# A fused two-block network: the second half of each weight unit becomes a plain difference, one unit in six moves to GpSimd, and a unit's first products come first

## The chip, the core and the metric

The kernel runs on one core of one Trainium2 chip. A core has five engines that run side by side, each through its own list of instructions in a fixed order: TensorE (PE, matrix products; its weight loads are shown apart as PEld), VectorE (DVE), ScalarE (ACT), GpSimd (POOL) and SyncE (SP, which here only issues transfers). They wait for each other on semaphores. SBUF is the on-chip memory of 128 partitions, PSUM the eight banks into which TensorE adds up products. The metric is the time of one execution on the device in microseconds.

## The reference

The program computes two transformer-like blocks on 256 tokens of width 2048, in float32. The large work is dense products with weights that are read once from HBM; between them stand small per-head products.

```python
# first block (one layer)
h = rms_norm(x, ln1); proj = h @ w_in                  # 2048 x 15376
y_a = gated_deltanet(...) @ w_branch_a                 # 8 heads of 128, chunks
y_b = moba_attention(...) @ w_branch_b                 # softmax attention, 8 heads
x = x + (sigmoid(gate_a) * y_a + sigmoid(gate_b) * y_b) @ w_out
u = causal_dwconv(rms_norm(x, ln2) @ w_up, ffn_conv, bias)
x = x + (silu(u_gate) * u_val) @ w_down; x = rms_norm(x, final_norm)
# second block (two layers)
shift, scale, gate = split(silu(c) @ w_mod[l] + b_mod[l])
h = rmsnorm(x) * (1 + scale) + shift; proj = h @ w_in_2[l]
y = concat(sparse_attention(...) * silu(g_a), groupnorm(retention(...)) * silu(g_b)) @ w_out_2[l]
x = x + gate * y
```

## The kernel before, in words

**Units.** Every dense product W·x is cut into blocks of 512 output columns and these into units of 128 x 1024 weights (`CH`), some 800 in all. A unit's path: SyncE starts a transfer of 512 KB into a slot of `ring` (or into a lent part of `AR` or `X`). ScalarE writes the rounded first half, `w1 = round(128 W)`, into a slot named `w` (`scalar_program.split`, recorded at L1431). VectorE writes the second half, `w2 = round(129 W - w1)`, over the raw weights (`vector_program.split`, recorded at L1881 as `ring_r<-ring,w`). TensorE then takes 16 products of 256 columns (orientation CM, weights stationary) or 8 of 512 (TM, activations stationary).

**Two products in place of one.** The fast float32 form of TensorE (`fp32r`, tiles named `_r`) rounds its inputs. So both operands are split in two: the activations into `x1 = round(x / 129)` and `x2 = x - 128 x1` (`first` and `second`; in `hhi`/`hlo` for the normed input), the weights into `w1` and `w2`. The block's sum is the sum of x1·w1 and x2·w2. In `gemm_part` the two products of one tile stand next to each other, first x1·w1, then x2·w2, and the unit begins with a wait for `w2_done`.

**Order of the work.** A planner in Python writes one list `steps` (sends, splits, units, phases of small jobs) and every engine runs its part in that order. Splits are put as far ahead as slots allow (`look_ahead`: 6 slots for `w1`, 9 for raw weights, plus lent ones). Between units come the phases of small jobs, a set number of units apart (`PAUSES`), and 192 units of `w_mod` for the second block's modulation, which VectorE alone multiplies and adds (`macc<-ring,sm,macc`, 128x1024).

**Small jobs that the change touches.** *Attention* (`moba` 4 jobs, `sparse` 8 jobs of two heads each): VectorE takes the row sums' reciprocals, ScalarE scales four identities by them (`inverse_sums`, `stg<-cst,sm`), and TensorE transposes and divides at once by six plain float32 products per job (`attend`, `ps<-stg,AR`). *Gated delta rule* (`gdn`, 4 jobs): TensorE spreads the cumulative decay and `bk` over rows (eight products), ScalarE copies the second to SBUF (`br`), GpSimd multiplies the matrix `AT` by it (`at`, recorded at L2478), and a doubling scheme inverts a triangular matrix. GpSimd also serves the masks of `gdn` (`AR<-AR,lev`), the relative-position bias (`AR<-AR` 128x1024 int32), rotary sums and the indexer.

## Time and profile before

| | us |
|---|---|
| median of 3 runs | 1954.91 (1953.28 to 1960.38) |
| the profiled execution's own time | 1957.05 |
| its span, first to last instruction | 1955.2 |
| PE busy | 1857.7 (95%) |
| PEld busy | 1738.3 (89%) |
| DVE busy | 1698.6 (87%) |
| ACT busy | 1233.6 (63%) |
| POOL busy | 228.9 (12%) |
| read from HBM | 531.50 MB, 273 GB/s over the span |

Busy time is the time in which an engine has at least one instruction under way. Products overlap in TensorE's pipeline (a product of 256 columns is drawn 0.28 us long while the next starts after 0.12 us), so TensorE's pace is read from starts and not from durations. A plain float32 product is recorded as two matmuls, an `fp32r` product or a transpose as one. A helper's line stands for all its uses: L151 is every product, L1431 every ScalarE copy, L1881 every three-operand VectorE instruction, L2478 every two-operand GpSimd instruction. All instructions of one name are then told apart by their tiles and shapes.

### The profile page before, as it was taken

What the parts mean: (1) busy time and instruction counts of PE and PEld (TensorE: products, weight loads), DVE (VectorE), ACT (ScalarE), POOL (GpSimd) and SP (SyncE); (2) the same over time, 40 slices, a digit from 0 to 9 for tenths busy, and PEclk for the clock granted to TensorE, in tenths of its full rate; (3) what the DMA queues carried; (4) which work ended last, traced back from release to release, by engine and by line L of the source; (5) the groups of instructions that cost most, each with busy time, mean ns of one, the idle gap of its engine ahead of it and who ended that gap; (6) DMA issues with size and microseconds to landing.
All of it is one profiled execution on the core that took longest, in us unless ns stands there. A gap on an engine that the chain in (4) does not pass through costs nothing.

```text
span 1955.2 us, 33776 instructions
## 1 busy us (share of the span) xinstructions
PE 1857.7 (95%) x13206; PEld 1738.3 (89%) x13206; DVE 1698.6 (87%) x2200; ACT 1233.6 (63%) x1911; POOL 228.9 (12%) x144
## 2 busy tenths in 40 slices
PE   6999999999999999899999999899999989998998
PEld 5888799999997899889998997898888879988887
DVE  7887997988798799999999997898888889897886
ACT  6667654744664674656765666755667775656773
POOL 0000041042010001222000000042210003232000
PEclk9999998999999999899999999999999999999999
DMA  8887776868898897688989997777788868786985
GB/s 287 261 271 248 258 241 218 286 211 276 302 356 318 283 309 241 223 289 294 318 308 344 331 328 244 273 255 255 246 267 307 272 222 301 227 278 209 331 290 183
DMA packets 258523, 535.82 MB, mean 274 GB/s; under 512 B 23608, under 2 KB 28733, under 8 KB 257341
## 3 DMA queue, kind: packets, MB, share of 16 engines
q1 hardware_dynamic: 257933, 531.44, 80.2%
q8 instruction: 105, 1.72, 0.3%
q10 hardware_dynamic: 432, 2.23, 0.3%
q14 instruction: 53, 0.43, 0.1%
HBM read 531.50 MB, written 2.10 MB: 273 GB/s over the span
## 4 chain that ended last, share of the span: by engine, by line
PE 41%; DVE 13%; ACT 5%; issue 4%; POOL 1%; DMA 1%; ACTq 0%; DVEq 0%; SPq 0%
PE ps L151 41%; DVE ring_r L1881 4%; ACT w L1431 2%; DVE macc L1881 2%; DVE AR_r L1881 1%; POOL AR L2478 1%; DMA ring<-in_w_in 1%; ACT stg L1437 1%; DVE stg L1873 1%; DVE AR L1873 1%; DVE stg L1881 1%; DVE AR L1881 1%; ACT L1437 1%; DVE stg L1878 0%; ACT stg L1431 0%
## 5 line engine op out<-in xcount | busy, mean ns | idle before, releaser
L151 PE MATMUL ps<-hh_r,w 128*128 128x256 f32 (+1 forms) x3500 | 865.5, 288 | 12.0 <-DVE ring_r L1881 6.8
L151 PE MATMUL ps<-hlo,ring_r 128*128 128x256 f32 x3116 | 758.9, 285 | 0.0
L1881 DVE SCALAR_TENSOR_TENSOR ring_r<-ring,w 128x1024 fp32r<-128x1024 f32 x495 | 621.5, 1275 | 115.6 <-ACT w L1431 114.4
L151 PEld LDWEIGHTS ps<-hh_r,w 128*128 128x128 f32 (+1 forms) x3500 | 671.2, 192 | 19.3 <-DVE ring_r L1881 8.1
L1431 ACT ACTIVATE w<-ring 128x1024 fp32r<-128x1024 f32 x495 | 511.3, 1055 | 179.0 <-PE ps L151 84.7
L151 PEld LDWEIGHTS ps<-hlo,ring_r 128*128 128x128 f32 x3116 | 596.7, 192 | 0.9 <-issue 0.5
L151 PE MATMUL ps<-w,AR_r 128*128 128x512 f32 x608 | 240.2, 395 | 2.7 <-DVE AR_r L1881 2.7
L151 PE MATMUL ps<-hlo,AR_r 128*128 128x256 f32 (+1 forms) x900 | 223.9, 287 | 0.0
L1881 DVE SCALAR_TENSOR_TENSOR AR_r<-AR,w 128x1024 fp32r<-128x1024 f32 (+1 forms) x150 | 187.7, 1262 | 34.0 <-ACT w L1431 33.6
L151 PE MATMUL ps<-ring_r,AR_r 128*128 128x512 f32 x520 | 203.8, 392 | 0.0
L151 PE MATMUL ps<-AR 128*128 128x64 f32 (+5 forms) x1340 | 182.7, 298 | 21.2 <-DVE AR L1877 10.9
L151 PEld LDWEIGHTS ps<-AR 128*128 128x128 f32 (+1 forms) x1340 | 166.8, 198 | 31.2 <-issue 15.9
L1431 ACT ACTIVATE w<-AR 128x1024 fp32r<-128x1024 f32 (+1 forms) x150 | 154.3, 1045 | 59.9 <-PE ps L151 34.2
L1881 DVE SCALAR_TENSOR_TENSOR macc<-ring,sm,macc 128x1024 f32<-128x1024 f32 x130 | 176.3, 1356 | 1.2 <-DMA ring<-in_w_mod 1.2
L151 PEld LDWEIGHTS ps<-hlo,AR_r 128*128 128x128 f32 (+1 forms) x900 | 174.1, 193 | 0.1
L2478 POOL TENSOR_TENSOR AR<-AR,stg 128x512 f32<-128x512 f32 (+1 forms) x41 | 66.2, 1632 | 734.2 <-DVE stg L1878 568.3
L151 PE MATMUL ps<-AR_r 128*128 128x512 f32 (+1 forms) x480 | 149.9, 363 | 0.0
L151 PE MATMUL ps<-hh_r,AR_r 128*128 128x256 f32 (+1 forms) x596 | 149.0, 288 | 0.9 <-DVE hlo L1881 0.9
L151 PEld LDWEIGHTS ps<-w,AR_r 128*128 128x128 f32 x608 | 115.0, 189 | 26.9 <-DVE ring_r L1881 2.5
L151 PEld LDWEIGHTS ps<-ring_r,AR_r 128*128 128x128 f32 x520 | 98.5, 190 | 20.1
L151 PEld LDWEIGHTS ps<-hh_r,AR_r 128*128 128x128 f32 (+1 forms) x596 | 114.1, 191 | 2.5 <-issue 2.3
L1881 DVE SCALAR_TENSOR_TENSOR ring_r<-ring,AR_r 128x1024 fp32r<-128x1024 f32 x81 | 104.6, 1293 | 13.2 <-ACT AR_r L1431 13.0
(223 smaller groups left out, 2475.4 us busy)
## 6 DMA issues: line engine op xcount, KB each, us to landing
ring<-in_w_in SPq DMA_DIRECT2D x314, 512.0 KB, 5.0
ring<-in_w_mod SPq DMA_DIRECT2D x141, 512.0 KB, 5.8
ring<-in_w_up SPq DMA_DIRECT2D x126, 512.0 KB, 5.5
ring<-in_w_down SPq DMA_DIRECT2D x66, 512.0 KB, 5.9
ring<-in_w_out SPq DMA_DIRECT2D x64, 512.0 KB, 5.5
AR<-in_w_in SPq DMA_DIRECT2D x63, 512.0 KB, 5.4
AR<-in_w_up SPq DMA_DIRECT2D x50, 512.0 KB, 5.4
AR<-in_w_mod SPq DMA_DIRECT2D x38, 512.0 KB, 5.9
```

The source lines that it names most:

```text
L151: return e.matmul(o, l, x, start=start, stop=stop, skip_group_check=True)
L1431: return e.activation(o, i, ACT.Copy, scale=scale)
L1437: return e.activation(o, i, f, scale=scale, **kw)
L1873: return e.tensor_tensor(o, a, b, op)
L1881: return e.scalar_tensor_tensor(o, a, s, b, op0, op1)
L2478: return e.tensor_tensor(o, a, b, op)
```

## The change

- The factor 129 (`SPK`) leaves the weights. ScalarE writes `w1 = round(128/129 W)`; the second half is the plain difference `w2 = W - w1`, a two-operand instruction. The activations carry the factor instead: the constants in the normalisations, in `gdn`, `moba`, `up`, `glu` and the residual are multiplied by it.
- Of the units of weights one in six (`i % SHARE == 3`) gets its second half from GpSimd, under a semaphore of its own (`w2_pool`), except around a block whose input is fresh (`fresh`: from two units ahead of it to nine behind its start). The changed program has 110 such instructions, all of 128x1024.
- `gemm_part` runs all first products of a unit, then waits for the second half and runs all second products.
- Attention: ScalarE divides the exponentials in place (`divided`), and TensorE transposes them against the identity, six single-pass transposes per job.
- `gdn`: the `bk` rows, ScalarE's copy `br` and GpSimd's product `at` go; `AT` is scaled by `bk` where VectorE forms it, and VectorE's preparations on two to four columns are rearranged.

```diff
 # tensor_program, gemm_part
-            e.wait_ge(*w2_done.after(j))
+            e.wait_ge(*w1_done.after(j))
...
                     for i in range(2):
-                        o, a = ps[i][:, 0:n], slice(128 * i, 128 * i + 128)
-                        fp(o, x1[:, a], b1[:, kk, :], k == 0, False)
-                        q = fp(o, x2[:, a], b2[:, kk, :], False, end)
+                        fp(ps[i][:, 0:n], x1[:, 128 * i:128 * i + 128], b1[:, kk, :], k == 0, False)
...
+            e.wait_ge(*(w2_pool if j in on_pool else w2_done).after(j))
+            for kk in range(m):
...
+                        q = fp(ps[i][:, 0:n], x2[:, 128 * i:128 * i + 128], b2[:, kk, :], False, end)
...
 # scalar_program, split
-            copy(wslot[j].at[:, 0:n], slot[j].at[0][:, 0:n], scale=SPL).then_inc(*w1_done.step(j))
+            copy(wslot[j].at[:, 0:n], slot[j].at[0][:, 0:n], scale=SPL / SPK).then_inc(*w1_done.step(j))
 # vector_program, split
+            if j in on_pool:
+                return
             e.wait_ge(*w1_done.after(j))
-            stt(rounded[:, 0:n], raw[:, 0:n], SPL + 1.0, wslot[j].at[:, 0:n], MUL, SUB).then_inc(*w2_done.step(j))
+            tt(rounded[:, 0:n], raw[:, 0:n], wslot[j].at[:, 0:n], SUB).then_inc(*w2_done.step(j))
 # GpSimd's program
+        def split(j):
...
+            if j in on_pool:
+                e.wait_ge(*w1_done.after(j))
+                tt(rounded[:, 0:n], raw[:, 0:n], wslot[j].at[:, 0:n], SUB).then_inc(*w2_pool.step(j))
 # planner
+    units = [j for j, c in enumerate(chunks) if c[0] == "w"]
+    fresh = [i for i, j in enumerate(units) if chunks[j][1]["fresh"] and chunks[j][2] == 0]
+    on_pool = {j for i, j in enumerate(units) if i % SHARE == 3 and all(not f - 2 <= i < f + 10 for f in fresh)}
 # attend (TensorE), inverse_sums -> divided (ScalarE)
-                fp(b0[:, 256 * h:256 * h + 128], L0[:, h, :], r0)
+                e.transpose(b0[:, 256 * h:256 * h + 128], L0[:, h, :], ident)
...
-            for u in range(4):
-                q = copy(quarter(st(J, "s"), u), ident, scale=rcol[:, u:u + 1])
+            for h in range(2):
+                copy(L0[:, h, :], L0[:, h, :], scale=rcol[:, h:h + 1])
+                q = copy(L1[:, h, :], L1[:, h, :], scale=rcol[:, 2 + h:3 + h])
 # gdn: TensorE, ScalarE, GpSimd
-                for u, h, n, c in G.U:
-                    q = fp(quarter(b, u), G.bk[:, u:u + 1].to_broadcast([128, 128]), ident)
...
-                copy(flat2(G.PP), b[:, :]).then_inc(*gdn_act.step("br", bt))
...
-                tt(flat2(G.AT), flat2(G.AT), flat2(G.PP), MUL).then_inc(*gdn_pool.step("at", bt))
```

TensorE at the program's first unit, bank by bank (`ps0`, `ps1` are the two banks of the block; `hh_r` is x1, `hlo` is x2, `w1` the first half, `ring_r` the second). Before:

```order
L151 MATMUL ps0<-hh_r,w1 128x256
L151 MATMUL ps0<-hlo,ring_r 128x256
L151 MATMUL ps0<-hh_r,w1 128x256
L151 MATMUL ps0<-hlo,ring_r 128x256
L151 MATMUL ps1<-hh_r,w1 128x256
L151 MATMUL ps1<-hlo,ring_r 128x256
L151 MATMUL ps1<-hh_r,w1 128x256
L151 MATMUL ps1<-hlo,ring_r 128x256
```

The same unit now:

```order
L152 MATMUL ps0<-hh_r,w1 128x256 x2
L152 MATMUL ps1<-hh_r,w1 128x256 x2
L152 MATMUL ps0<-hh_r,w1 128x256 x2
L152 MATMUL ps1<-hh_r,w1 128x256 x2
L152 MATMUL ps0<-hlo,ring_r 128x256 x2
L152 MATMUL ps1<-hlo,ring_r 128x256 x2
L152 MATMUL ps0<-hlo,ring_r 128x256 x2
L152 MATMUL ps1<-hlo,ring_r 128x256 x2
```

The count is the same; eight products now stand ahead of the first that needs the second half, and two products in a row no longer add to the same sum.

VectorE in the feed-forward stage, about 829 to 857 us of the trace before (`macc` is the modulation, `X<-ps,X` the half sums, `AR<-AR,cst` a step of the bias). Before:

```order
L1881 SCALAR_TENSOR_TENSOR AR_r<-AR,w 128x1024 x2
L1881 SCALAR_TENSOR_TENSOR ring_r<-ring,w 128x1024 x3
L1881 SCALAR_TENSOR_TENSOR macc<-ring,sm,macc 128x1024
L1881 SCALAR_TENSOR_TENSOR ring_r<-ring,AR_r 128x1024
L1881 SCALAR_TENSOR_TENSOR X<-ps,X 128x512 x2
L1877 TENSOR_SCALAR AR<-AR,cst 128x1024
L1881 SCALAR_TENSOR_TENSOR ring_r<-ring,w 128x1024 x3
```

Now:

```order
L1888 TENSOR_TENSOR AR_r<-AR,w 128x1024 x2
L1888 TENSOR_TENSOR ring_r<-ring,w 128x1024 x2
L1896 SCALAR_TENSOR_TENSOR macc<-ring,sm,macc 128x1024
L1888 TENSOR_TENSOR ring_r<-ring,AR_r 128x1024
L1896 SCALAR_TENSOR_TENSOR X<-ps,X 128x512 x2
L1892 TENSOR_SCALAR AR<-AR,cst 128x1024
L1888 TENSOR_TENSOR ring_r<-ring,w 128x1024 x2
```

Two of nine second halves have left VectorE's list here; the rest keeps its place.

GpSimd from the end of the merge (`stg<-stg,X`) into the feed-forward stage, the 12 bias steps being `AR<-AR` 128x1024. Before:

```order
L2478 TENSOR_TENSOR stg<-stg,X 128x512 x8
L2513 MEMSET AR 128x8
L2514 MEMSET AR 128x32
L2478 TENSOR_TENSOR AR<-AR 128x1024 x12
L2478 TENSOR_TENSOR AR<-AR,stg 128x256
```

Now:

```order
L2496 TENSOR_TENSOR ring_r<-ring,w 128x1024 x2
L2528 MEMSET AR 128x8
L2529 MEMSET AR 128x32
L2496 TENSOR_TENSOR ring_r<-ring,w 128x1024 x2
L2496 TENSOR_TENSOR AR_r<-AR,w 128x1024
L2496 TENSOR_TENSOR AR<-AR 128x1024
L2496 TENSOR_TENSOR ring_r<-ring,w 128x1024
L2496 TENSOR_TENSOR AR<-AR 128x1024
L2496 TENSOR_TENSOR AR_r<-AR,w 128x1024
L2496 TENSOR_TENSOR AR<-AR 128x1024
L2496 TENSOR_TENSOR ring_r<-ring,w 128x1024
```

The second halves stand between the bias steps, and each waits in GpSimd's list behind the step ahead of it.

## Rows read from the trace of the kernel before

**Rows 1.** The page: busy time of each engine; the chain that ended last, by engine.
```profile
PE 1857.7 (95%) x13206; PEld 1738.3 (89%) x13206; DVE 1698.6 (87%) x2200; ACT 1233.6 (63%) x1911; POOL 228.9 (12%) x144
PE 41%; DVE 13%; ACT 5%; issue 4%; POOL 1%; DMA 1%; ACTq 0%; DVEq 0%; SPq 0%
```

**Rows 2.** Busy time by stage: feed-forward; second block, layer one; layer two.
```profile
core 0: us, PE busy (x) PEld busy (x) DVE busy (x) ACT busy (x) POOL busy (x), PEclk, DMA share, GB/s
...
690.00:1160.00 470.00, 459.01 (x3333) 438.10 (x3332) 442.78 (x526) 294.97 (x397) 42.16 (x12) 0.98 0.86 298
1200.00:1550.00 350.00, 330.79 (x2344) 306.58 (x2343) 302.80 (x407) 237.34 (x403) 53.28 (x31) 0.97 0.79 263
1600.00:1900.00 300.00, 281.88 (x2085) 264.66 (x2084) 263.92 (x354) 201.68 (x341) 53.58 (x31) 0.98 0.81 269
```

**Rows 3.** Waits of TensorE: who for whom, us in total, times, longest.
```profile
PE ps L1088 <- DMA AR<-in_gdn_conv: 12.1, 1, 12.1
PE ps L151 <- ACT stg L1431: 8.3, 4, 2.5
PE ps L151 <- DVE ring_r L1881: 8.1, 4, 5.0
PE ps L151 <- DVE AR_r L1881: 7.3, 5, 3.1
```

**Rows 4.** Waits of VectorE, same columns.
```profile
DVE ring_r L1881 <- ACT w L1431: 114.4, 105, 3.8
```

**Rows 5.** Second halves on VectorE: count, min/median/max ns, first and last start.
```profile
L1881 DVE SCALAR_TENSOR_TENSOR ring_r<-ring,w x495: 1204/1222/2921, 16.4 to 1930.7; 128x1024 fp32r<-128x1024 f32 x165
```

**Rows 6.** In order of time, VectorE, then GpSimd: start, us, instruction.
```profile
450.35 1.22 DVE L1881 SCALAR_TENSOR_TENSOR ring_r<-ring,w 128x1024 fp32r<-128x1024 f32 x1
451.48 2.19 DVE L1881 SCALAR_TENSOR_TENSOR AR_r<-AR,w 128x1024 fp32r<-128x1024 f32 x1
453.59 2.18 DVE L1881 SCALAR_TENSOR_TENSOR macc<-ring,sm,macc 128x1024 f32<-128x1024 f32 x1
...
450.94 3.75 POOL L2478 TENSOR_TENSOR AR<-AR,lev 128x512 f32<-128x512 f32 x2 [4.23 <-PE ps L151]
```

**Rows 7.** The same, where VectorE reads PSUM meanwhile.
```profile
315.01 4.38 DVE L1881 SCALAR_TENSOR_TENSOR AR<-ps,VT,AR 128x253 f32<-128x253 f32 x11 [0.40 <-ACT AR L1431]
...
315.02 2.29 POOL L2478 TENSOR_TENSOR AR<-AR,lev 128x512 f32<-128x512 f32 x2 [5.72 <-PE ps L151]
```

**Rows 8.** The same in the feed-forward stage, GpSimd 1024 wide.
```profile
807.84 4.05 DVE L1881 SCALAR_TENSOR_TENSOR ring_r<-ring,w 128x1024 fp32r<-128x1024 f32 x2
...
792.79 6.21 POOL L2478 TENSOR_TENSOR AR<-AR 128x1024 int32<-128x1024 int32 x1 [21.68 <-DVE AR L1877]
808.00 2.81 POOL L2478 TENSOR_TENSOR AR<-AR 128x1024 int32<-128x1024 int32 x1 [9.00 <-DVE AR L1877]
```

**Rows 9.** TensorE in order of time: plain float32 products, then transposes.
```profile
237.73 3.62 PE L151 MATMUL ps<-AR 128*128 128x128 f32 x31
...
243.05 0.60 PE L1229 MATMUL ps<-cst,AR 128*128 128x128 f32 x4
243.49 0.60 PE L1232 MATMUL ps<-cst,AR 128*128 128x128 f32 x4
```

**Rows 10.** ScalarE: the four scaled identities; one pass over 256 columns.
```profile
1336.07 0.49 ACT L1437 ACTIVATE AR<-AR,sm 128x256 f32<-128x256 f32 x1
...
1340.05 1.27 ACT L1431 ACTIVATE stg<-cst,sm 128x128 f32<-128x128 f32 x4 [1.57 <-DVE sm L2071]
```

**Rows 11.** TensorE inside a unit, in order of time.
```profile
700.84 0.28 PE L151 MATMUL ps<-hh_r,w 128*128 128x256 f32 x1
700.96 0.28 PE L151 MATMUL ps<-hlo,AR_r 128*128 128x256 f32 x1
701.08 0.28 PE L151 MATMUL ps<-hh_r,w 128*128 128x256 f32 x1
```

**Rows 12.** GpSimd: groups by form; count, busy us, mean ns, idle before.
```profile
L2478 POOL TENSOR_TENSOR AR<-AR 128x512 f32<-128x512 f32 x5 | 7.4, 1476 | 311.2 <-DVE AR L1881 311.1
```

More of the change, by code:

```diff
@@ L167, with pauses @@
 }
+PLACES = {}
+SHARE = 6
+MODS = {}
+def pauses(job):
+    return PLACES.get((job.kind, *job.at), PAUSES.get(job.kind, ()))
 USES = {
@@ L443, in inline @@
         job = Job(kind, *at)
-        for seg in range(len(PAUSES.get(kind, ())) + 1):
+        for seg in range(len(pauses(job)) + 1):
             phase(job, seg)
     def enqueue(q, jobs, seg=0):
-        q.append([[(j, s, (PAUSES[j.kind] + (0,))[s]) for j in jobs
-                   for s in range(seg, len(PAUSES[j.kind]) + (j is jobs[-1]))],
-                  PAUSES[jobs[0].kind][seg - 1] if seg and PAUSES[jobs[0].kind] else 0])
+        q.append([[(j, s, (pauses(j) + (0,))[s]) for j in jobs
+                   for s in range(seg, len(pauses(j)) + (j is jobs[-1]))],
+                  pauses(jobs[0])[seg - 1] if seg and pauses(jobs[0]) else 0])
     def step_jobs():
@@ L598, in evacuate @@
                 enqueue(short, [job], 2)
-            elif kind != "ga" and len(PAUSES.get(job.kind, ())) > 0:
+            elif kind != "ga" and len(pauses(job)) > 0:
                 enqueue(short, [job], 1)
@@ L1066, in gemm_part @@
                 k = k0 + kk
-                end = k == kt - 1
                 if b["fresh"] and (k % 2 == 0):
@@ L1081, in gemm_part @@
                         fp(o, b1[:, kk, a], x1, k == 0 and ct % 2 == 0, False)
+            e.wait_ge(*(w2_pool if j in on_pool else w2_done).after(j))
+            for kk in range(m):
+                k = k0 + kk
+                end = k == kt - 1
+                x1, x2 = operand(b, k + b["k0"])
+                if b["orient"] == "TM":
+                    for i in range(2):
+                        q = fp(ps[i][:, 0:n], x2[:, 128 * i:128 * i + 128], b2[:, kk, :], False, end)
+                else:
+                    for ct in range(-(-n // 128)):
+                        a = slice(128 * ct, min(128 * ct + 128, n))
+                        o = ps[ct // 2][0:a.stop - a.start, 256 * (ct % 2):256 * (ct % 2) + 256]
                         q = fp(o, b2[:, kk, a], x2, False, end)
@@ L1567, in moba @@
             if seg == 3:
-                inverse_sums(J, rcol, moba_dve.after("recip", hp), moba_act.step("diag", hp))
+                divided(L0, L1, rcol, moba_dve.after("recip", hp), moba_act.step("diag", hp))
             if seg == 4:
@@ L1575, in moba @@
                 e.wait_ge(*moba_pe.after("pv", hp))
-                copy(st(J, "s"), pb(J, "f")[:, :]).then_inc(*moba_act.step("out", hp))
+                copy(st(J, "s"), pb(J, "f")[:, :], scale=SPK).then_inc(*moba_act.step("out", hp))
                 e.wait_ge(*moba_act.after("out", hp))
@@ L1658, in gdn @@
                 e.wait_ge(*gdn_dve.after("qk3", bt))
-                for u in range(4):
-                    q = copy(G.KX[:, u, :], quarter(b, u), scale=G.ksc[:, u:u + 1])
+                for u, h, n, c in G.U:
+                    q = copy(G.KX[:, u, :], quarter(b, u), scale=eg[:, 1, h:h + 1] if n else G.ksc[:, u // 2:u // 2 + 1])
                 q.then_inc(*gdn_act.step("kx3", bt))
@@ L1806, in sparse @@
             if seg == 3:
-                inverse_sums(J, rcol, sp_dve.after("recip", L, hp), sp_act.step("diag", L, hp))
+                divided(L0, L1, rcol, sp_dve.after("recip", L, hp), sp_act.step("diag", L, hp))
             if seg == 4:
@@ L1988, in rstd @@
                 e.wait_ge(*rstd_dve.after("gain0", n))
-                ts(gsp, gsc, 1.0 / (SPL + 1.0), MUL)
-                ts(shp, modcm[:, L, 0:16], 1.0 / (SPL + 1.0), MUL).then_inc(*rstd_dve.step("gain", n))
+                ts(gsp, gsc, 1.0 / SPK, MUL)
+                ts(shp, modcm[:, L, 0:16], SPK, MUL).then_inc(*rstd_dve.step("gain", n))
             e.wait_ge(*sumsq.after("sq", 4 if n == 2 else n, 1, 3))
@@ L2111, in bd_job @@
                 ts(gcn, two(pb(J, "b")[:, 0:16]), -1.0, MUL).then_inc(*bd_dve.step("gcn"))
-                e.wait_ge(*bd_act.after("eg"))
-                tt(beg, bet[:, 1, :], eg[:, 1, :], MUL).then_inc(*bd_dve.step("beg"))
         def conv(J, seg):
@@ L2139, in conv @@
                 e.wait_ge(*conv_act.after("root", *J.at))
[L2140 removed]
+                root = st(J, "z")[:, 0:4] if kind == "q" else krt[:, 4 * hp:4 * hp + 4]
+                e.reciprocal((rq if kind == "q" else rk)[:, 4 * hp:4 * hp + 4], root).then_inc(*conv_dve.step("inv", *J.at))
         def z_silu(J, seg):
@@ L2563, in pool_program @@
         for what, *a in steps:
-            if what == "phase" and a[0].kind in parts:
+            if what == "split":
+                split(*a)
+            elif what == "phase" and a[0].kind in parts:
                 parts[a[0].kind](*a)
```

81 lines of the change are left out of this document (38 added, 43 removed).

## Prediction

> **What bounds the kernel now.** I read the page first: TensorE is busy for 1857.7 of 1955.2 us, VectorE for 1698.6, and the chain that ended last runs for 41% through products and for 13% through VectorE [rows 1]. So there is a first engine with little idle time (97.5 us) and a second that is not far behind it. The reader is to see both numbers: a gain has to come out of TensorE's work or its waits, and a loss can come from VectorE. Then the stages: in the feed-forward stage VectorE is busy for 442.8 of 470 us, in the two layers of the second block for 302.8 of 350 and 263.9 of 300 [rows 2]. VectorE has 27.2, 47.2 and 36.1 us left there, about 6% in the first and 12% in the others.
>
> Then TensorE's waits. Waits for `ring_r`, which are those for a second half, are 8.1 us in 4 times; those for `AR_r` are 7.3 us in 5 times, and that name is also carried by activations [rows 3]. The largest single one, 12.1 us, is the start of the program, which the change does not touch [rows 3]. Seen from the other side, VectorE itself waited 105 times, 114.4 us in all, for ScalarE's first half before it could form a second one [rows 4]: most second halves are formed as early as the slots allow and lie ready before TensorE comes to them. The pace inside a unit: starts at 700.84, 700.96, 701.08, 0.12 us per product of 256 columns, no matter whether the next one adds to the same sum or to another [rows 11].
>
> **The plain difference.** The three-operand form takes 1222 ns at the median [rows 5], and the next 1024-wide one starts 1.13 us after it (450.35, 451.48) [rows 6]. The two-operand form of 128x1024 is not in the trace. It reads the same two tensors and writes the same one. Bounds: half the price at the one end (0.57 us, as if a pass were saved, which would take another 0.57 us from each of the 690 that stay on VectorE), 1.28 us at the other, the price of the other three-operand form beside it. The nearest row is the three-operand form itself, so I take its price: a difference of 0 us. ScalarE's instruction has another constant, 0 us. The factors in the activations sit in constants of instructions that stand there anyway, 0 us.
>
> **First products first.** No instruction comes or goes; TensorE may start a unit when the first half is there, and reaches the wait eight products later, 8 x 0.12 = 0.95 us [rows 11]. Only a unit that waited for its second half gains, at most 0.95 us: 4 such waits for `ring_r` give 3.8 us, and if all 5 of `AR_r` were second halves it would be 8.6 us [rows 3]. I take 4. It adds a wait in the middle of a unit; behind it on TensorE stands only the unit itself, and after it the small jobs that stood behind the unit before. Should alternating between sums have cost something, the pace would change; the rows show 0.12 us for both kinds of step, so 0.
>
> **Attention.** Twelve jobs with six plain float32 products each. The trace draws such a product as two matmuls, and 31 of them in a row take 3.62 us, so (3.62 - 0.28)/30 = 0.111 us apart [rows 9]. Transposes: four from 243.05, the next kind from 243.49, 0.11 us each, drawn once [rows 9]. So a job goes from 12 x 0.111 = 1.33 us to 6 x 0.11 = 0.66 us, and twelve save 8.0 us. ScalarE had four scaled identities in 1.27 us, 0.3 us apart [rows 10]; now it has two passes over 128 columns and two over 256 (0.49 us, 0.4 apart): 1.5 us, and TensorE, which waited 8.3 us in 4 times for them [rows 3], may wait 0.2 us longer each time. 12 x 0.2 = 2.4 us on ScalarE, which is busy for 63% of the span [rows 1]; less than 1 us of it counts.
>
> **Gated delta rule.** 16 broadcasts of `bk` go, 32 matmuls x 0.111 = 3.6 us of TensorE. Four `at` products on GpSimd go, of the kind that takes 1476 ns on average [rows 12], with four copies on ScalarE. They stand in a chain of dependent steps; if VectorE and TensorE come to the next step 1 us sooner in each job, that is 4 us. It lies between 0 (the step comes at its place in the list anyway) and 4 x 1.5 = 6; I take 4 with the broadcasts counted apart.
>
> TensorE's work thus falls by 8.0 + 3.6 = 11.6 us.
>
> **One unit in six on GpSimd.** 110 second halves leave VectorE: 110 x 1.13 = 124 us of its work. What GpSimd takes is the unknown. It takes 2.29 us for two products of 512 columns while VectorE reads PSUM, 1.15 each [rows 7]. Where VectorE reads two SBUF tensors it is another picture: GpSimd needs 3.75 us for two, and the VectorE instructions at 451.48 and 453.59 take 2.19 and 2.18 us in place of 1.22 and about 1.28 [rows 6]: VectorE stands still for 0.9 to 0.97 us while GpSimd has the inputs. At 1024 columns (int32) GpSimd takes 2.81 us, and two second halves that run beside it take 4.05 us, where 1.13 + 1.22 = 2.35 is the price alone: 1.7 us of standstill [rows 8]. So a 1024-wide difference on GpSimd would hold VectorE for 1.7 (the int32 row) to 1.94 us (twice the 512-wide 0.97), if VectorE comes with a two-tensor instruction just then, and for nothing if VectorE is idle or reads PSUM. Per unit VectorE's time changes by -1.13 at one end and by 1.94 - 1.13 = +0.81 us at the other; times 110 this is -124 to +89 us. VectorE is busy for 87% of the span and most of its work has two SBUF inputs, so I take three quarters of 1.94, 1.46 us, +0.33 per unit, +36 us. Of this only what falls on stretches in which VectorE is on the path counts, 13% of the span by the chain [rows 1]: about 5 us, and 6 with the worse timing of the small jobs. The other 30 us go into VectorE's idle time, of which the 114.4 us of [rows 4] are a part; without that cover they would all count.
>
> The Trainium skill has this as a rule and it speaks against the change: "SBUF — State Buffer", section "Who interferes with whom", says that a VectorE instruction with two SBUF inputs and a GpSimd instruction that reads SBUF exclude each other, and that the later one stands still for the whole of the other. The rows above agree in kind (0.97 and 1.7 us of standstill) [rows 6, 8]. The skill's "GPSIMD Engine Reference", section "Elementwise — side-by-side cycle accounting", gives 4497 ns for 2048 columns; an estimate from it for 1024 is 2.25 us, by which the worst case per unit would be +1.12 us and the whole +123 us of VectorE's time. The sum does not use it.
>
> A second cost: GpSimd can also come late. At 792.79 one step took 6.21 us instead of 2.81, since VectorE's instructions followed one another without a gap [rows 8]. The unit's second half is then ready some 5 to 6 us after the first. TensorE needs it later than that where the slots are full, so I count nothing; it is in rival A.
>
> **Sum.** -11.6 (products) - 4 (waits for second halves) - 4 (gated delta rule) + 6 (VectorE) = -13.6 us. Against the profiled execution's own 1957.05 us that is 1943.4; its time lies 2.1 us above the median of the three runs, 1954.91, so on their scale 1941.3, 0.7% less. What a measurement of this kernel can tell from no change I take as 0.5%, 9.8 us: 1945.1 and 1964.7 are the bounds.
>
> **Rivals.**
>
> A, slower: the standstill of VectorE decides. In the feed-forward stage some 37 units go to GpSimd; at the full +0.81 they add 30 us to a VectorE that has 27.2 us left [rows 2], and since the load comes in bunches I count 10 us. In the two layers of the second block 57 units add 46 us, of which half lands where TensorE waits for small jobs: 23 us. With the 19.6 us of gains it comes to 1955 + 33 - 19.6 = 1968, and to 1975 if late second halves add some. For it: [rows 6, 8]. Against: TensorE waits for a second half only a few times now [rows 3], so there is room. It decides once VectorE's work per stage passes the stage's length.
>
> B, a larger gain: TensorE's small-job waits come from a VectorE that is behind, and 110 instructions fewer in its list bring it forward. Of 97.5 us of idle time 85 are not the start; and the granted clock is 0.97 to 0.98 in the stages [rows 2], a 2% loss on 1955 us, some 40 us, that follows on idle time. A third of both is 28 + 13 = 41 us; with the 11.6 of products 1955 - 53 = 1902, say 1905. For it: the standstill is zero where VectorE is idle or reads PSUM [rows 7]. Against: most of VectorE's list reads two SBUF tensors.
>
> C, no difference: the products removed lie where TensorE waits for others anyway (41% of the chain is TensorE [rows 1]), so 5 of the 11.6 us count, the waits' 4 and the delta rule's 4 are eaten by VectorE's +8: 1955 - 5 = 1950.
>
> Chances: my forecast (1925 to 1945) 0.35; B 0.17; C (1945 to 1965) 0.25; A 0.23. So faster by over 0.5% 0.52, within 0.5% 0.25, slower 0.23. The range takes in B's number and A's 1975: 1903 to 1976; the likeliest case's own range is 1925 to 1945.
>
> **What would show it.** The products: `ps<-stg,AR` gone, 72 transposes in its place, each 0.11 us after the last. The price: TENSOR_TENSOR `ring_r<-ring,w` with a median of 1222 ns; a median well below overturns my zero. The standstill: its mean above its median, single ones at 3 us, and GpSimd instructions of 2.3 us alone and over 3 beside VectorE; VectorE's busy time near 1698.6 + 36 = 1735 us. If it falls below 1650, the 0.33 is wrong and B is near. TensorE's waits for `ring_r`: a few us at most. If they are over 20 us, or if a GpSimd-made second half heads the list of TensorE's waits, A holds. A pace other than 0.12 us inside a unit would make all of this wrong, as it would count some 12,000 times (800 units of 16 or 8 products).

## The result, and the profile after

| | before | after |
|---|---|---|
| median, us | 1956.35 (1953.28 to 1960.38, 4 runs) | 2010.96 (2010.05 to 2012.02, 4 runs) |
| ratio after to before | | 1.0278, 95% interval 1.0257 to 1.0299 |
| span of the profiled execution | 1955.2 | 2009.2 |
| mean granted clock of TensorE | 0.977 | 0.959 |

The change makes the kernel 54.6 us slower, where 13.6 us less was forecast. The page of the changed kernel, busy times and then the chain that ended last (they answer to [rows 1]):

```profile
PE 1868.5 (93%) x13102; PEld 1743.9 (87%) x13102; DVE 1723.1 (86%) x2089; ACT 1232.3 (61%) x1907; POOL 527.3 (26%) x250
PE 38%; DVE 15%; ACT 5%; issue 4%; POOL 3%; DMA 1%; ACTq 0%; DVEq 0%
```

Each page is of one execution. TensorE has 104 instructions fewer and is busy 10.8 us longer, at a lower granted clock; its idle time grew from 97.5 to 140.7 us. VectorE has 111 instructions fewer and is busy 24.5 us longer, yet its share of the span fell from 87 to 86%. The stages (same columns as [rows 2]; since the kernel is slower, the same stretch holds somewhat less work):

```profile
690.00:1160.00 470.00, 450.60 (x3224) 429.67 (x3224) 438.37 (x480) 287.43 (x388) 129.45 (x45) 0.97 0.83 285
1200.00:1550.00 350.00, 317.03 (x2172) 289.46 (x2173) 296.89 (x383) 223.94 (x388) 102.81 (x50) 0.95 0.76 253
1600.00:1900.00 300.00, 278.19 (x1975) 256.44 (x1974) 256.84 (x331) 191.12 (x327) 100.65 (x48) 0.98 0.78 254
```

VectorE is busy for 438, 297 and 257 of 470, 350 and 300 us: it has idle time in all three stages. TensorE's waits in the changed kernel (us in total, times, longest; they answer to [rows 3]):

```profile
PE ps L152 <- DVE macc L1896: 17.6, 6, 4.5
PE ps L1174 <- ACT AR L1452: 17.4, 5, 6.4
PE ps L152 <- DVE AR L1892: 16.9, 3, 9.1
PE ps L1113 <- DMA AR<-in_gdn_conv: 12.1, 1, 12.1
PE ps L152 <- ACT w L1452: 10.4, 4, 4.6
PE ps L1423 <- DVE stg L1888: 10.2, 5, 5.7
PE ps L152 <- DVE sm L2189: 7.2, 1, 7.2
```

The waits for `ring_r` are nearly gone (1.3 us, once). What grew are waits for small jobs: the end of the modulation (`macc`, 6.7 us before), the divided exponentials (`L1174`; 14.4 us in 6 times in the kernel without the share, which is introduced below), the bias and mask steps (`AR L1892`, 10.9 us in 2 times before). TensorE hardly waits for the second half of a unit; it waits for small jobs that stand behind second halves in VectorE's list.

The second halves themselves (count, min/median/max ns, first and last start), on VectorE and on GpSimd, beside [rows 5]:

```profile
L1888 DVE TENSOR_TENSOR ring_r<-ring,w x425: 1187/1217/3444, 16.4 to 1983.0; 128x1024 fp32r<-128x1024 f32 x142
L2496 POOL TENSOR_TENSOR ring_r<-ring,w x70: 2356/2691/7601, 50.5 to 1984.9; 128x1024 fp32r<-128x1024 f32 x70
```

The median is that of before (1217 against 1222 ns), the longest is 3444 ns. In order of time, VectorE and then GpSimd (start, us), to be read beside [rows 6]:

```profile
1005.63 4.58 DVE L1888 TENSOR_TENSOR ring_r<-ring,w 128x1024 fp32r<-128x1024 f32 x2
...
1006.17 2.95 POOL L2496 TENSOR_TENSOR ring_r<-ring,w 128x1024 fp32r<-128x1024 f32 x1 [11.02 <-ACT w L1452]
```

GpSimd comes in the middle of VectorE's first instruction, waits until it ends (2.95 in place of 2.36 us), and VectorE's second one stands still until GpSimd is done: the two take 4.58 us where 1.22 + 1.13 = 2.35 is their price, 2.2 us of standstill.

And what such a delay meets. The longest of TensorE's waits that grew is one for a bias step in the feed-forward stage. GpSimd, VectorE and TensorE in the changed kernel:

```profile
771.62 3.32 POOL L2496 TENSOR_TENSOR ring_r<-ring,w 128x1024 fp32r<-128x1024 f32 x1
...
772.66 2.82 DVE L1892 TENSOR_SCALAR AR<-AR,cst 128x1024 f32<-128x1024 int32 x1
...
775.63 3.59 PE L152 MATMUL ps<-AR 128*128 128x32 f32 x16 [9.11 <-DVE AR L1892]
```

The same step in the kernel without the share:

```profile
751.16 0.74 DVE L1892 TENSOR_SCALAR AR<-AR,cst 128x1024 f32<-128x1024 int32 x1
...
752.05 3.10 PE L152 MATMUL ps<-AR 128*128 128x32 f32 x16 [3.99 <-DVE AR L1892]
```

GpSimd's second half makes the step 2.1 us longer (2.82 against 0.74), and TensorE waits for just this step. It waits 5.1 us more in all; for the other 3 us VectorE came later to this place against TensorE, behind two more holds (a `ring_r` and a `macc` that started at 745.89 and 751.17 us).

A second place shows another way of being late. It is the longest wait for the divided exponentials, one attention job of the second block's first layer: VectorE, GpSimd, ScalarE and TensorE, each in order of time:

```profile
1392.28 3.42 DVE L1896 SCALAR_TENSOR_TENSOR macc<-AR,sm,macc 128x1024 f32<-128x1024 f32 x1
1395.62 1.75 DVE L1888 TENSOR_TENSOR AR_r<-AR,AR_r 128x1024 fp32r<-128x1024 f32 x1
1398.66 1.39 DVE L1896 SCALAR_TENSOR_TENSOR AR<-ps,sm,AR 128x128 f32<-128x128 f32 x4 [1.29 <-POOL AR L2496]
...
1402.30 1.00 DVE L1899 TENSOR_REDUCE sm<-AR 128x2 f32<-128x256 f32 x2
1403.33 0.17 DVE L1892 TENSOR_SCALAR sm<-sm 128x4 f32<-128x4 f32 x1
...
1391.24 3.38 POOL L2496 TENSOR_TENSOR ring_r<-ring,w 128x1024 fp32r<-128x1024 f32 x1
1394.58 3.95 POOL L2496 TENSOR_TENSOR AR<-AR,sel 128x256 f32<-128x256 f32 x2
...
1403.54 0.40 ACT L1458 ACTIVATE AR<-AR,sm 128x128 f32<-128x128 f32 x1 [9.67 <-DVE sm L1892]
...
1409.37 0.44 PE L1174 MATMUL ps<-cst,AR 128*128 128x128 f32 x1 [6.39 <-ACT AR L1452]
1409.60 0.42 PE L1175 MATMUL ps<-cst,AR 128*128 128x128 f32 x1
```

In the kernel without the share the same job reads:

```profile
1353.29 1.76 DVE L1896 SCALAR_TENSOR_TENSOR macc<-AR,sm,macc 128x1024 f32<-128x1024 f32 x1
1354.97 2.31 DVE L1888 TENSOR_TENSOR AR_r<-AR,AR_r 128x1024 fp32r<-128x1024 f32 x1
1357.21 1.21 DVE L1888 TENSOR_TENSOR ring_r<-ring,w 128x1024 fp32r<-128x1024 f32 x1
1358.34 1.38 DVE L1896 SCALAR_TENSOR_TENSOR AR<-ps,sm,AR 128x128 f32<-128x128 f32 x4
...
1352.24 3.96 POOL L2496 TENSOR_TENSOR AR<-AR,sel 128x256 f32<-128x256 f32 x2
...
1363.21 0.40 ACT L1458 ACTIVATE AR<-AR,sm 128x128 f32<-128x128 f32 x1 [6.51 <-DVE sm L1892]
...
1369.04 0.45 PE L1174 MATMUL ps<-cst,AR 128*128 128x128 f32 x1 [4.01 <-ACT AR L1452]
```

GpSimd's second half at 1391.24 makes the `macc` take 3.42 us, 2.1 more than its price. But here the hold is made good: VectorE has one second half less to form, and in the kernel without the share GpSimd's own product `AR<-AR,sel` holds the same two VectorE instructions (1.76 and 2.31 us). What is left is that this product now stands behind the second half in GpSimd's list and starts 3.4 us later against VectorE's `macc`, and VectorE waits for it for 1.29 us. From the `macc` to `AR<-ps,sm,AR` VectorE takes 6.38 us, and 5.05 without the share: this wait is the whole delay. Behind it stand the maxima (`TENSOR_REDUCE`), for whose result ScalarE sits idle, then the exponentials, the reciprocals and ScalarE's division, and TensorE waits for 6.39 us in place of 4.01. The rest of that difference is that TensorE came to the wait about 1 us sooner. So a share on GpSimd also delays GpSimd's own small jobs; what that is worth over the whole kernel is bounded below.

The reader is to see that VectorE can be late although it is busy for 86% only: its free time lies elsewhere. TensorE's last two rows also show its pace behind a wait of several us: the transposes start 0.23 us apart, where they are 0.11 apart in undisturbed jobs.

### The profile page after: what moved, and what is told of

The parts are those of the page before. It is cut to its first block, busy times and chain, and to the rows that moved or that the text cites. A ratio compares the mean times of both kernels' runs of the same rounds, so it can differ in the third digit from the quotient of the medians.

```text
span 2009.2 us, 33543 instructions
## 1 busy us (share of the span) xinstructions
PE 1868.5 (93%) x13102; PEld 1743.9 (87%) x13102; DVE 1723.1 (86%) x2089; ACT 1232.3 (61%) x1907; POOL 527.3 (26%) x250
## 4 chain that ended last, share of the span: by engine, by line
PE 38%; DVE 15%; ACT 5%; issue 4%; POOL 3%; DMA 1%; ACTq 0%; DVEq 0%
PE ps L152 38%; DVE ring_r L1888 4%; POOL AR L2496 2%; DVE macc L1896 2%; ACT w L1452 2%; DVE stg L1896 2%; DVE AR_r L1888 1%; DVE stg L1888 1%; ACT stg L1458 1%; DVE AR L1888 1%; DVE AR_r L1896 1%; DVE AR L1896 1%; DMA ring<-in_w_in 1%; ACT L1458 1%; DVE AR L1892 0%
## 5 line engine op out<-in xcount | busy, mean ns | idle before, releaser
L1888 DVE TENSOR_TENSOR ring_r<-ring,w 128x1024 fp32r<-128x1024 f32 x425 | 579.5, 1380 | 108.0 <-ACT w L1452 107.2
L152 PE MATMUL ps<-hh_r,w 128*128 128x256 f32 (+1 forms) x3500 | 511.5, 290 | 7.1 <-ACT w L1452 5.6
L152 PEld LDWEIGHTS ps<-hh_r,w 128*128 128x128 f32 (+1 forms) x3500 | 460.6, 194 | 15.1 <-ACT w L1452 7.2
L152 PE MATMUL ps<-hlo,ring_r 128*128 128x256 f32 x3116 | 442.0, 285 | 1.3 <-DVE ring_r L1888 1.3
L2496 POOL TENSOR_TENSOR ring_r<-ring,w 128x1024 fp32r<-128x1024 f32 x70 | 205.1, 2929 | 834.9 <-ACT w L1452 834.9
L152 PEld LDWEIGHTS ps<-hlo,ring_r 128*128 128x128 f32 x3116 | 405.8, 192 | 2.0 <-DVE ring_r L1888 1.9
L1888 DVE TENSOR_TENSOR AR_r<-AR,w 128x1024 fp32r<-128x1024 f32 (+1 forms) x128 | 181.2, 1426 | 36.2 <-ACT w L1452 36.1
L152 PE MATMUL ps<-hlo,AR_r 128*128 128x256 f32 (+1 forms) x900 | 128.5, 286 | 0.2 <-DVE AR_r L1888 0.2
L1888 DVE TENSOR_TENSOR ring_r<-ring,AR_r 128x1024 fp32r<-128x1024 f32 x74 | 104.2, 1411 | 17.3 <-ACT AR_r L1452 17.2
L1452 ACT ACTIVATE AR_r<-ring 128x1024 fp32r<-128x1024 f32 x81 | 85.2, 1055 | 31.8 <-PE ps L152 20.1
```

The source lines that it names most:

```text
L152: return e.matmul(o, l, x, start=start, stop=stop, skip_group_check=True)
L1452: return e.activation(o, i, ACT.Copy, scale=scale)
L1888: return e.tensor_tensor(o, a, b, op)
L2496: return e.tensor_tensor(o, a, b, op)
```

## The experiments

Theory 1: GpSimd's share costs the time, because it holds VectorE. Rivals: the order of products (2), the smaller jobs (3), and, within the share, that GpSimd's halves come late (1b). A narrower form of theory 1 is that a hold costs only where small jobs on VectorE stand in TensorE's way (1c). "Against before" is the median less that of the kernel before in the same batch. VectorE's busy time and TensorE's idle time (span less busy time) are from each one's profiled execution.

| run | against before, us | ratio, 95% interval | VectorE busy | TensorE idle |
|---|---|---|---|---|
| changed kernel | +54.6 | 1.0278 (1.0257 to 1.0299) | 1723.1 | 140.7 |
| no share | +1.0 | 1.0007 (0.9993 to 1.0021) | 1694.1 | 107.2 |
| share, old order | +58.0 | 1.0295 (1.0273 to 1.0316) | 1720.5 | 147.1 |
| no share, old order | +4.9 | 1.0021 (1.0010 to 1.0032) | 1694.0 | 111.7 |
| write only | -37.1 | 0.9806 (0.9792 to 0.9821) | 1568.7 | 84.3 |
| hold only | +94.7 | 1.0480 (1.0467 to 1.0494) | 1833.2 | 173.8 |
| added on VectorE | +69.4 | 1.0351 (1.0334 to 1.0369) | 1810.0 | 152.9 |
| one input | -19.5 | 0.9903 (0.9888 to 0.9917) | 1611.0 | 93.2 |
| quarters | +22.5 | 1.0122 (1.0107 to 1.0137) | 1689.9 | 123.8 |
| one in twelve | +18.0 | 1.0093 (1.0080 to 1.0106) | 1706.8 | 119.3 |
| calm stretches | +27.8 | 1.0148 (1.0132 to 1.0164) | 1719.9 | 123.7 |
| attention only | +1.9 | 1.0004 (0.9992 to 1.0016) | 1697.9 | 104.7 |
| transposes undivided | -0.9 | 0.9999 (0.9988 to 1.0010) | 1698.0 | 103.3 |
| delta rule only | +0.8 | 1.0006 (0.9998 to 1.0015) | 1695.0 | 104.2 |
| order only | -2.5 | 0.9982 (0.9973 to 0.9991) | 1698.4 | 98.5 |

**Share and order, two by two.**

```diff
-    on_pool = {j for i, j in enumerate(units) if i % SHARE == 3 and all(not f - 2 <= i < f + 10 for f in fresh)}
+    on_pool = set()
```

> The changed kernel, but VectorE forms every second half; all other edits stay. Theory 1 (GpSimd's share costs the time: its instructions hold VectorE, and the small jobs behind them come late to TensorE): the other terms of the prediction are left, so 1956.4 - 19.6 = 1937 us, between 1930 and 1950; VectorE's second halves have mean and median together near 1.25 us. Theory 2 (the order of the products inside a unit costs it, by late second halves or a worse stream on TensorE): still above 1990. Theory 3 (the smaller attention and delta-rule jobs start something later): still above 1990.

Without the share the kernel is at 1957.66 us: 53.6 of the 54.6 us belong to the share. The 19.6 us of other gains are missing too, which none of the theories had, so the time lies above the range of 1930 to 1950.

```diff
             e.wait_ge(*w1_done.after(j))
+            e.wait_ge(*(w2_pool if j in on_pool else w2_done).after(j))
...
-                        fp(ps[i][:, 0:n], x1[:, 128 * i:128 * i + 128], b1[:, kk, :], k == 0, False)
+                        o, a = ps[i][:, 0:n], slice(128 * i, 128 * i + 128)
+                        fp(o, x1[:, a], b1[:, kk, :], k == 0, False)
+                        q = fp(o, x2[:, a], b2[:, kk, :], False, end)
...
-            e.wait_ge(*(w2_pool if j in on_pool else w2_done).after(j))
...
```

> The changed kernel with the product order of before (first and second product of a tile next to each other, the unit waits for its second half at its start); GpSimd keeps its 110 units. Theory 1: 2011 or some us more, up to 2025, since GpSimd's late second halves now hold the whole unit. Theory 2: near 1955.

> The changed kernel without GpSimd's share and with the product order of before: only the plain difference, the constants and the smaller jobs are left. Theory 1: as without the share alone, plus the 4 us that the order was to bring, 1941 (1933 to 1953). Theory 2: 1940 too, but then the run without the share and with the new order is at 1990. Theory 3: above 1990.

The old order costs 3.4 us more with the share and 3.9 without: theory 2 falls. So does theory 3, since neither kernel without the share is near 1990. What is left without share and order (plain difference, constants, smaller jobs) was to bring 15.6 us and brings none: the kernel is 4.9 us slower than before.

**Hold or lateness.** In the first run GpSimd keeps its place, its waits and its signal, and reads nothing:

```diff
-                tt(rounded[:, 0:n], raw[:, 0:n], wslot[j].at[:, 0:n], SUB).then_inc(*w2_pool.step(j))
+                e.memset(rounded[:, 0:n].bitcast(F32), 0.0).then_inc(*w2_pool.step(j))
```

> The changed kernel, but GpSimd writes zeros to its 110 units' second half in place of the difference: it reads no SBUF; same place in its list, same wait, same signal. (What it leaves out: those units' second half of the weights.) Theory 1, in the form that VectorE's standstill costs the time: VectorE is not held and has 110 instructions less than without the share (1957.7), so 1957 or less, 1935 to 1960; VectorE's second halves beside GpSimd take 1.22 us. Theory 1b, GpSimd's halves come late (its place in the list, its waits): still above 1990.

1920.47 us, below even the range of 1935 to 1960: taking 110 second halves off VectorE is worth 38 us when nothing holds it. The changed kernel, which differs from this run in what GpSimd reads and in how long its instruction is, is 90.5 us slower (91.7, each against its own before). VectorE and GpSimd of the write-only run, at a place like the one above:

```profile
684.50 2.36 DVE L1888 TENSOR_TENSOR ring_r<-ring,w 128x1024 fp32r<-128x1024 f32 x2
...
685.45 0.96 POOL L2581 MEMSET ring_r<- 128x1024 f32 x1 [9.20 <-ACT w L1452]
```

Two second halves in 2.36 us with GpSimd's instruction across both: no standstill. In the second run VectorE forms all halves, and GpSimd reads at the same places for nobody:

```diff
+    on_pool = set()
+    extra = {j for i, j in enumerate(units) if i % SHARE == 3 and all(not f - 2 <= i < f + 10 for f in fresh)}
...
 # GpSimd's program
+            if j in extra:
                 e.wait_ge(*w1_done.after(j))
...
+                tt(spare[:, :].rearrange("p (a b) -> p a b", b=256), mid(cst[:, 0:256], 4), mid(cst[:, 0:256], 4), ADD).then_inc(*w2_pool.step(j))
```

> The changed kernel with every second half on VectorE, and at the 110 places GpSimd adds two tensors of 128x1024 (a constant, into a spare 16-bit buffer that nobody reads): the hold without relief and without lateness. If the hold of VectorE costs the time, it must be at or above the changed kernel's 2011, since 110 x 1.22 = 134 us of VectorE's work have come back as well: 2030 to 2100, VectorE's busy time above 1800. If lateness of GpSimd's halves is the cause: 1958, as without the share.

2052.27 us. No other engine waits for the result of these additions, so none of this is a late second half (1b): 110 two-input instructions on GpSimd that relieve nobody cost 93.7 us against the kernel without the share. GpSimd's own later jobs can still come late in this run. The third run puts the same instruction on VectorE:

```diff
 # vector_program, behind its own second half, in place of GpSimd's program
+            if j in extra:
...
+                tt(spare[:, :].rearrange("p (a b) -> p a b", b=256), mid(cst[:, 0:256], 4), mid(cst[:, 0:256], 4), ADD).then_inc(*w2_pool.step(j))
```

> The changed kernel without the share, and at the same 110 places VectorE adds a constant into the spare 16-bit buffer (128x1024), as GpSimd did in the run of the hold alone: the same load on VectorE as its own work, without a hold. 110 x 1.1 to 1.3 us = 121 to 143 us more of VectorE's time. If a us of standstill costs no more than a us of work: as the hold alone per us, 0.68 x 130 = 88: 2045 us, 2030 to 2060. If only the standstill is dear and work costs what relief gave (0.28): 1957 + 36 = 1993, 1985 to 2005.

The added instruction, on GpSimd in the run of the hold, then on VectorE:

```profile
L2496 POOL TENSOR_TENSOR spare<-cst 128x1024 bf16<-128x1024 f32 x110 | 342.7, 3116 | 1183.5 <-ACT w L1454 1070.1 <-ACT AR_r L1454 88.3 <-ACT X_r L1454 25.0
```

```profile
L1890 DVE TENSOR_TENSOR spare<-cst 128x1024 bf16<-128x1024 f32 x110 | 137.1, 1247 | 0.0
```

2026.69 us, between the two expectations. Per us of VectorE's busy time, from the kernel without the share: relief 38.1 / 125.4 = 0.30, hold 93.7 / 139.1 = 0.67, own work 68.4 / 115.9 = 0.59. From there a held us is little dearer than a worked one. From the write-only kernel it is another matter: to form the 110 halves on VectorE again costs the same 0.30, and GpSimd's hold in the changed kernel 91.7 / 154.4 = 0.59. So there is no single rate. For own work and for hold alike it is higher where VectorE already carries more, and in the changed kernel the held us cost twice what the relieved ones gave.

**What GpSimd reads, and how long its instruction is.**

```diff
-                tt(rounded[:, 0:n], raw[:, 0:n], wslot[j].at[:, 0:n], SUB).then_inc(*w2_pool.step(j))
+                e.tensor_scalar(rounded[:, 0:n], raw[:, 0:n], 0.0, None, MUL).then_inc(*w2_pool.step(j))
```

> The changed kernel, but GpSimd forms raw x 0 in place of the difference: one SBUF input and not two, same width. (What it leaves out: the second half of the 110 units.) If every read of GpSimd holds a VectorE instruction with two SBUF inputs: GpSimd's instruction takes 1.2 to 2.4 us, VectorE is held as long, and the time lies between 1957 and 2011, near 1985. If only the instruction with two inputs does: as with writing alone, 1920 (1915 to 1928), and VectorE's second halves beside it take 1.22 us.

```diff
-                tt(rounded[:, 0:n], raw[:, 0:n], wslot[j].at[:, 0:n], SUB).then_inc(*w2_pool.step(j))
+                for p in range(4):
+                    a = slice(p * n // 4, (p + 1) * n // 4)
+                    q = tt(rounded[:, a], raw[:, a], wslot[j].at[:, a], SUB)
+                q.then_inc(*w2_pool.step(j))
```

> The changed kernel, but GpSimd forms each of its 110 second halves in four instructions of 128x256. If the length of one hold decides: VectorE is held for 0.6 us at a time and small jobs come through between: 1965 to 1995. If the sum of the holds decides: 2005 to 2030, a little more than the changed kernel's 2011 by the start of each instruction.

VectorE and GpSimd of each, first one input, then quarters:

```profile
705.70 2.06 DVE L1888 TENSOR_TENSOR ring_r<-ring,w 128x1024 fp32r<-128x1024 f32 x1
...
705.30 3.12 POOL L2581 TENSOR_SCALAR ring_r<-ring 128x1024 fp32r<-128x1024 f32 x1 [9.68 <-ACT w L1452]
```

```profile
714.60 1.76 DVE L1888 TENSOR_TENSOR ring_r<-ring,w 128x1024 fp32r<-128x1024 f32 x1
716.28 1.75 DVE L1896 SCALAR_TENSOR_TENSOR macc<-AR,sm,macc 128x1024 f32<-128x1024 f32 x1
717.96 3.42 DVE L1888 TENSOR_TENSOR AR_r<-AR,w 128x1024 fp32r<-128x1024 f32 x2
...
714.19 6.10 POOL L2496 TENSOR_TENSOR ring_r<-ring,w 128x256 fp32r<-128x256 f32 x4 [7.47 <-ACT w L1452]
```

One input: VectorE stands still for 0.84 us and not for the whole 3.12, and the time, 1938.7, is near neither number. This run also bounds how much of the loss can be GpSimd's own small jobs coming late behind its halves. GpSimd is busy for 552.3 us here and for 527.3 in the changed kernel, so its list is as late, and yet the run is only 17.6 us slower than the write-only one, VectorE's 42.3 us of hold included. So about that much of the 91.7 us, at most, is lateness of GpSimd's own jobs, unless it costs more beside a VectorE that is held longer, which no run separates; the rate of the hold would then be (91.7 - 17.6) / 154.4 = 0.48, still above 0.30. A second sign is that VectorE and ScalarE wait 42.0 us for GpSimd in the changed kernel, 30.9 without the share, and 42.2 in the run with the addition on VectorE, where GpSimd has no added work at all.

Quarters: the four pieces come between VectorE's instructions, each of which takes 0.5 us longer; VectorE's busy time is 33.2 us less than with whole instructions, and the time 1979.84, 31 us less, inside the range for the length of one hold. But total and length fell together, so this run does not tell them apart. TensorE also waits 7.0 us for GpSimd's quarters (7 times), which it did not for its whole halves. The run shows that a held us spread thin is not free either (59.6 us over the write-only run for 121.2 us of hold). It also points to held time being dearer than own work: VectorE is busy about as long as without the share (1689.9 and 1694.1 us), and the kernel is 21.5 us slower, of which those waits for the quarters are a part.

**How many, and where.**

```diff
-SHARE = 6
+SHARE = 12
```

> The changed kernel with one unit in twelve on GpSimd in place of one in six, some 55 units. If each unit costs the same on balance (0.49 us: 53.7 us between the changed kernel and the one without the share, for 110 units): 1957 + 27 = 1984 us, 1978 to 1990. If the loss is a threshold that only the full share passes (rival A's point from which it decides): 1957 to 1965.

```diff
-    on_pool = {j for i, j in enumerate(units) if i % SHARE == 3 and all(not f - 2 <= i < f + 10 for f in fresh)}
+    calm = (*range(160, 190), *range(430, 470), *range(640, 705))
+    on_pool = {j for i, j in enumerate(units) if i in calm and i % 2 == 0 and all(not f - 2 <= i < f + 10 for f in fresh)}
```

> The changed kernel, but GpSimd gets every second unit in three stretches in which the changed kernel lost nothing against the one without the share (units 160 to 189, 430 to 469, 640 to 704), 56 units in all, and none elsewhere. Theory 1c (the hold costs only where small jobs on VectorE stand in TensorE's way): 1957 to 1962. If every unit costs by the count (55 units in the run with one in twelve: 16.8 us): 1970 to 1985.

The stretches were chosen by comparing the starts of the 800 first halves on ScalarE in the changed kernel and in the one without the share: across them the distance grew by 0.0, 1.6 and -0.3 us. 55 units at one in twelve cost 17.0 us against the kernel without the share, 0.31 each; 110 at one in six cost 53.6, 0.49 each; 56 at one in two in the three "calm" stretches cost 26.8, 0.48 each. One in twelve fits neither number: no threshold, but less than in proportion. Theory 1c falls in the form that was tested: these stretches were nearly free at one in six, not at one in two. That the slack of VectorE takes a few holds and then no more fits both runs; it was not tested by itself.

**The smaller jobs, one by one, on the kernel before.**

```diff
-                fp(b0[:, 256 * h:256 * h + 128], L0[:, h, :], r0)
...
+                e.transpose(b0[:, 256 * h:256 * h + 128], L0[:, h, :], ident)
...
 # ScalarE
-        def inverse_sums(J, rcol, need, sig):
...
+        def divided(L0, L1, rcol, need, sig):
...
```

> The kernel before with only the attention edit: ScalarE divides the exponentials, TensorE transposes them. The prediction's term: 12 x 0.66 = 8.0 us less on TensorE, under 1 us of it lost to ScalarE: 1949 (0.9963). The rival that the trace of the run without the share suggests (TensorE waits 14.4 us in 6 times for the divided exponentials): the gain is eaten, 0.998 to 1.003.

The same with ScalarE left as it was:

> The kernel before with TensorE's half of the attention edit alone: transposes in place of the products, while ScalarE goes on scaling the identities (which nobody multiplies by). (What it leaves out: the division by the row sums.) If the full edit gained nothing because ScalarE's division comes later to TensorE than its scaled identities did (13.8 us of waits in place of 8.3): the 8.0 us show here, 1949 to 1952, 0.996 to 0.998. If the products removed lay beside another wait anyway: 1957, 0.999 to 1.001.

```diff
-                    q = fp(quarter(b, u), G.bk[:, u:u + 1].to_broadcast([128, 128]), ident)
...
-                copy(flat2(G.PP), b[:, :]).then_inc(*gdn_act.step("br", bt))
...
-                tt(flat2(G.AT), flat2(G.AT), flat2(G.PP), MUL).then_inc(*gdn_pool.step("at", bt))
...
```

> The kernel before with only the gated-delta-rule edit (no rows of bk on TensorE, no copy on ScalarE, no product on GpSimd; VectorE's small preparations rearranged). The prediction's term: 3.6 of products and 4 of the chain, 7.6 us less: 1949 (0.9961). The rival: the steps come at their places in the list anyway, and the products lie beside other waits: 0.998 to 1.002. The run without share and in the old order was 4.9 us slower than before with both small-job edits and the plain difference in it; so at least one of the three must cost time: if attention gives -8 and this one -7.6, the plain difference costs some 20.

All three are at the time of before. TensorE's waits ahead of the transposes, with ScalarE's division and then without:

```profile
PE ps L1149 <- ACT AR L1430: 13.8, 6, 4.0
```

```profile
PE ps L1149 <- ACT stg L1430: 8.6, 4, 2.7
PE ps L1149 <- ACT AR L1430: 4.6, 1, 4.6
```

One job's scaled identities lie in `AR`, so both rows of the second run count: 13.8 us with the division and 13.2 without. The division is not what eats the gain. Without it the gain is missing as well: TensorE's busy time fell by 6.5 us (1857.7 to 1851.2) and its idle time rose by 5.8. In sum the products went, and TensorE was idle in their place.

**The order alone.**

```diff
 # the kernel before, gemm_part
-            e.wait_ge(*w2_done.after(j))
+            e.wait_ge(*w1_done.after(j))
...
+            e.wait_ge(*w2_done.after(j))
```

> The kernel before with the new order of products alone (all first products of a unit, then the wait, then all second ones). The pair of runs without the share gave -3.9 us for it, the pair with the share -3.7, the prediction's term was -4: 1953, 0.997 to 0.999. If those two differences were chance: 1957. It is also the version that may beat both kernels.

0.9982 (0.9973 to 0.9991): the one of the edits that pays, 2.5 us by the medians, 3.5 by the ratio. This version is faster than both kernels, than the one before by about 0.2%.

## Why the prediction was wrong

**The plain difference** was right at 0 (1217 against 1222 ns), as far as the instruction goes. The edit was not run alone. With it, its constants and both small-job edits together the kernel was 4.9 us slower (2 to 6 by the interval). The small-job edits gave +1.9 and +0.8 us, zero within their intervals; the rest stays without a named cause.

**First products first** was right: forecast -4, measured -3.9, -3.4 and -2.5 in three pairs. With the order alone the waits for `ring_r` and `AR_r`, 15.4 us before, fell to 3.0 us, and waits for the first half, which did not exist before, came to 8.3 us in 4 times.

**Attention, -8.0, and the delta rule, -7.6**: the prices were right (72 transposes, 0.11 us apart in most jobs), their worth was not. The step that failed is "TensorE's work thus falls by 11.6 us", put into the sum in full. TensorE's work did fall (without the share it is busy for 1844.0 us, 13.7 less), and its idle time rose by 9.7. Rival C named this and took TensorE's share of the chain, 41%, as its measure; the runs show 0 for both edits. TensorE's wait for the identities was also read too low: 3.1 us more, once, stand under the name `AR`.

**GpSimd's share, +6.** The load came out near the forecast: 1.46 us of hold per unit and +36 us of VectorE's time were taken; against the write-only run the hold is (1723.1 - 1568.7)/110 = 1.40, and VectorE is busy 29 us longer than without the share. In part that is luck: three quarters of 1.94 was a guess, and a full hold takes 2.1 to 2.2 us, more than the bound of 1.94. What failed is the step "only what falls on stretches in which VectorE is on the path counts, 13% of the span". It fails twice. First, the rate: an added us of VectorE costs 0.59 to 0.67 us, not 0.13, by which the 36 us would have cost 21 to 24. The share of a chain tells where the path runs now, not how much slack the rest has: with VectorE busy for 87%, six in ten of the added us reached the end. Secondly, the netting: 124 us of relief were set against 160 of hold and the difference was priced. They have different rates, 0.30 and 0.59. By the runs the account is 38.1 us gained by relief and 91.7 lost by the hold (changed kernel less write only), together +53.6. The gain of the relief was rival B's, and it was real; the hold cost more than twice as much.

**Rival A** had the mechanism and its sign, and 1968 to 1975 for 2011. Its point from which it decides was wrong: VectorE was full in no stage (438 of 470 us in the feed-forward one), and yet its hold decided. It also took the 19.6 us of gains as given; without the share the kernel was 1.0 us slower than before, so none of them came. Of the 58.0 us between the two profiled spans, with the share and without, 33.5 are idle time of TensorE and 24.5 longer busy time, while the granted clock went from 0.977 to 0.959. Nothing had been counted for the clock on the side of the loss. The second cost, late halves from GpSimd (7.6 us for one of them), was rightly counted at nothing: the waits for `ring_r` did not grow. What stands behind such a half in GpSimd's own list was not counted; it costs 1.3 us in the job shown, and 17.6 us at most in all by the one-input run.

The Trainium skill's rule that the prediction quotes ("SBUF — State Buffer", section "Who interferes with whom") also says that a GpSimd instruction that only writes does not contend: the write-only run agrees. That the later engine stands still for the whole of the other's instruction holds here for two inputs (2.2 us of standstill, 2.36 us the instruction) and not for one (0.84 of 2.8 us); there the measurement decides.

Open: why a us taken from VectorE is worth half of a us added, and why a held us seems dearer than a worked one. That TensorE or the transfers bind once VectorE is quicker would explain the first, but no run shows it.

## What to carry to other kernels

Work moved to an engine that blocks the one it relieves is two changes, not one net: price the relief and the block apart, each by a run (an instruction in the same place that reads nothing; the same instruction for nobody). The room for delay is not the idle time of a stage but the slack ahead of the small steps that others wait for: look at what stands before each of them, in VectorE's list and in that of the engine that takes the share. And products taken from the busiest engine need not shorten anything: here two such edits each brought nothing, since TensorE was idle in their place.

## What the runs showed of the hardware

- GpSimd's two-input difference of 128x1024 takes 2.36 us alone, and 7.60 where VectorE's instructions follow without a gap: four of them began after it, ran at their usual length, and the fifth was held (3.43 us). In the row at 1006.17 it got its turn at the first boundary; what decides between the two is open.

```profile
849.42 1.28 DVE L1896 SCALAR_TENSOR_TENSOR macc<-ring,sm,macc 128x1024 f32<-128x1024 f32 x1
850.62 2.35 DVE L1888 TENSOR_TENSOR AR_r<-AR,w 128x1024 fp32r<-128x1024 f32 x2
852.89 2.35 DVE L1888 TENSOR_TENSOR ring_r<-ring,w 128x1024 fp32r<-128x1024 f32 x2
855.16 3.43 DVE L1896 SCALAR_TENSOR_TENSOR macc<-ring,sm,macc 128x1024 f32<-128x1024 f32 x1
...
849.91 7.60 POOL L2496 TENSOR_TENSOR ring_r<-ring,w 128x1024 fp32r<-128x1024 f32 x1 [16.49 <-ACT w L1452]
```

- Writing zeros over 128x1024 takes GpSimd 0.95 us and holds nobody; a one-input pass takes 2.8 us and held VectorE for 0.84 us in the row shown.
- VectorE's pass with one SBUF tensor (`AR L1892`, 0.75 us alone) is held as well, here beside GpSimd's second half at 900.76, as in the row at 772.66; the prediction counted only instructions with two SBUF inputs:

```profile
901.23 2.89 DVE L1892 TENSOR_SCALAR AR<-AR,cst 128x1024 f32<-128x1024 int32 x1
```
